# Constant products on TensorE ahead of the transposes at the block boundaries

## The reference

```python
def first_block(x, ...):
    for l in range(2):
        x = layer_norm(ALPHA * x + 0.5 * swiglu(x, ffn1...), ln_g[l, 0], ln_b[l, 0])
        proj = x @ w_in[l]                       # then pooling, gated conv, neighbourhood attention
        y = concat([y_a, y_b, y_c]) @ w_out[l]
        x = layer_norm(ALPHA * x + y, ln_g[l, 1], ln_b[l, 1])
        x = layer_norm(ALPHA * x + 0.5 * swiglu(x, ffn2...), ln_g[l, 2], ln_b[l, 2])

def second_block(x, mem, ...):
    for l in range(2):
        x = x + 0.5 * rmsnorm(swiglu(rmsnorm(x, ng[0]), w_ffn_in[l, 0], w_ffn_out[l, 0]), ng[1])
        x = x + rmsnorm(mixer(rmsnorm(x, ng[2]), ...), ng[3])   # MLA, GLA, RWKV, gates, w_out
        x = x + rmsnorm(mem_attn(rmsnorm(x, ng[4]), mem, ...), ng[5])
        x = x + 0.5 * rmsnorm(swiglu(rmsnorm(x, ng[6]), w_ffn_in[l, 1], w_ffn_out[l, 1]), ng[7])
```

## Time and profile before

| what | value |
|---|---|
| median of 3 runs | 3088.74 us (3088.4 to 3089.52) |
| the profiled execution, its own time | 3089.14 us |
| its span on the chip | 3087.2 us |
| TensorE busy (matmul) | 2788.6 us, 90% |
| VectorE, ScalarE, GpSimd busy | 1583.1, 1287.9, 477.0 us |
| mean granted TensorE clock | 0.939 |

### The profile page before, as it was taken

One profiled execution on the slowest core, in us unless ns is written; L12 is line 12 of the kernel. 1 busy time (PEld: TensorE's weight loads), 2 busy tenths in 40 slices (PEclk: granted clock), 3 DMA queues, 4 the chain that ended last, 5 costly groups with the idle time before them and its releaser, 6 DMA issues.

```text
span 3087.2 us, 52843 instructions
## 1 busy us (share of the span) xinstructions
PE 2788.6 (90%) x21412; PEld 2564.5 (83%) x21412; DVE 1583.1 (51%) x2182; ACT 1287.9 (42%) x1830; POOL 477.0 (15%) x199
## 2 busy tenths in 40 slices
PE   7989899898989989888889898998988888989898
PEld 7978798797879879777779787987977777978898
DVE  5566555555655555532555525555553254552555
ACT  3435444343544434434523444444443452344443
POOL 0000000000000000033424650000003342465000
PEclk9989999898999989898999998998989899999999
DMA  7665465566446546532322544655652232254464
GB/s 233 184 163 157 123 185 175 171 183 164 151 125 188 170 148 186 166 94 82 94 72 70 184 130 136 184 163 155 186 165 89 82 103 63 78 183 123 143 184 129
DMA packets 622823, 445.06 MB, mean 144 GB/s; under 512 B 27904, under 2 KB 589344, under 8 KB 622176
## 3 DMA queue, kind: packets, MB, share of 16 engines
q1 hardware_dynamic: 622688, 443.09, 47.8%
HBM read 441.99 MB, written 1.05 MB: 144 GB/s over the span
## 4 chain that ended last, share of the span: by engine, by line
PE 85%; DVE 9%; ACT 3%; issue 1%; DMA 1%; POOL 0%; SPq 0%; DVEq 0%; ACTq 0%; POOLq 0%
PE ps L357 18%; PE ps L358 17%; PE ps L359 17%; PE ps L373 7%; PE ps L374 7%; PE ps L375 6%; PE ps L583 2%; PE ps L607 1%; PE ps L400 1%; PE ps L1365 1%; ACT w_hi L624 1%; PE ps L1172 1%; PE ps L1079 1%; PE ps L1355 1%; DVE zT L1507 1%
## 5 line engine op out<-in xcount | busy, mean ns | idle before, releaser
L357 PE MATMUL ps<-in_hi,w_hi 128*128 128x256 f32 x4352 | 1266.8, 291 | 63.9 <-POOL w_lo L818 31.0
L358 PE MATMUL ps<-in_lo,w_hi 128*128 128x256 f32 x4352 | 1252.2, 288 | 0.0
L359 PE MATMUL ps<-in_hi,w_lo 128*128 128x256 f32 x4352 | 1250.8, 287 | 0.0
L624 ACT ACTIVATE w_hi<-raw 128x1024 fp32r<-128x1024 f32 x788 | 832.2, 1057 | 964.0 <-PE ps L359 632.8
L818 DVE TENSOR_TENSOR w_lo<-raw,w_hi 128x1024 fp32r<-128x1024 f32 x594 | 727.9, 1225 | 761.2 <-ACT w_hi L624 760.4
L357 PEld LDWEIGHTS ps<-in_hi,w_hi 128*128 128x128 f32 x4352 | 857.3, 197 | 85.9 <-issue 34.1
L358 PEld LDWEIGHTS ps<-in_lo,w_hi 128*128 128x128 f32 x4352 | 857.4, 197 | 7.1 <-issue 0.5
L359 PEld LDWEIGHTS ps<-in_hi,w_lo 128*128 128x128 f32 x4352 | 856.0, 197 | 0.0
L818 POOL TENSOR_TENSOR w_lo<-raw,w_hi 128x1024 fp32r<-128x1024 f32 x194 | 476.5, 2464 | 2357.4 <-ACT w_hi L624 2356.5
L373 PE MATMUL ps<-w_hi,hid_hi 128*128 128x512 f32 x704 | 283.3, 402 | 31.6 <-DVE hid_lo L892 31.6
L374 PE MATMUL ps<-w_lo,hid_hi 128*128 128x512 f32 x704 | 282.1, 401 | 0.0
(11 more groups left out here) (301 smaller groups left out, 2694.9 us busy)
## 6 DMA issues: line engine op xcount, KB each, us to landing
raw<-in_w_ffn_in SPq DMA_DIRECT2D x176, 512.0 KB, 3.7
raw<-in_w_mix SPq DMA_DIRECT2D x112, 512.0 KB, 3.6
raw<-in_ffn_w_gate SPq DMA_DIRECT2D x88, 512.0 KB, 3.7
raw<-in_ffn_w_up SPq DMA_DIRECT2D x88, 512.0 KB, 3.7
raw<-in_ffn_w_down SPq DMA_DIRECT2D x88, 512.0 KB, 3.5
raw<-in_w_ffn_out SPq DMA_DIRECT2D x88, 512.0 KB, 3.5
raw<-in_w_in SPq DMA_DIRECT2D x40, 512.0 KB, 4.7
raw<-in_w_out SPq DMA_DIRECT2D x32, 512.0 KB, 3.6
```

Of the source, the lines that this page charges most:

```text
L357: nc.tensor.matmul(o, lh, rh, start=first, stop=False, **kw)
L358: nc.tensor.matmul(o, lh, rl, start=False, stop=False, **kw)
L359: return nc.tensor.matmul(o, ll, rh, start=False, stop=last, **kw)
L624: nc.scalar.activation(w_hi[:, e % SPLIT, :], raw[:, e % RAW, :], ACT.Copy).then_inc(sem("split_high"), 1)
```

## The change

`pe_warm(pe, n)` runs n products of `ones` by `ones` in fp32, 128 x 128 by 256 columns, into PSUM bank 5, which nobody reads. None of them waits for a semaphore or signals one. They stand behind the block's last product and ahead of the turn, or ahead of `layer_end` and behind it. Nothing else is changed; each count holds for each of the two layers of its stack.

```diff
--- before.py
+++ after.py
@@ -386,6 +386,13 @@
 
                         mm.then_inc(sem("rows_out"), 1)
                 mm.then_inc(sem("piece_used"), 1)
+
+        WARM_BANK = 5
+
+        def pe_warm(pe, n):
+
+            for _ in range(n):
+                nc.tensor.matmul(ps[:, WARM_BANK, 0:S], ones[:, 0:P], ones[:, :], start=True, stop=True)
 
         BY_TOKENS = [(t, d) for t in range(HALF) for d in range(2)]
         BY_COLUMNS = [(t, d) for d in range(2) for t in range(HALF)]
@@ -1603,6 +1610,7 @@
             with pe.Fori(0, LAYERS) as l:
                 pe_turn(pe, 0, x_tok, BY_COLUMNS, waits=False)
                 pe_ffn(pe, 0, E1_FFN1, C1_FFN1)
+                pe_warm(pe, 9)
                 pe_turn(pe, 0, x_tok, BY_COLUMNS)
                 pe_linear(pe, 0, E1_IN, [features] * 8 + [tokens] * 2, C1_IN, TOGETHER)
 
@@ -1629,13 +1637,17 @@
 
                 pe.wait_ge(sem("na_out"), NA_HEADS)
                 pe_rows(pe, E1_OUT, C1_OUT)
+                pe_warm(pe, 9)
                 pe_turn(pe, 1, x_tok, BY_COLUMNS)
                 pe_ffn(pe, 1, E1_FFN2, C1_FFN2)
+                pe_warm(pe, 12)
                 layer_end(pe, l + 1)
 
             with pe.Fori(0, LAYERS) as l:
+                pe_warm(pe, 5)
                 pe_turn(pe, 0, z_tok, BY_TOKENS)
                 pe_ffn(pe, 0, E_FFN1, C_FFN1)
+                pe_warm(pe, 15)
                 pe_turn(pe, 1, z_tok, BY_TOKENS)
                 pe_linear(pe, Q_IN, E_IN, [features] * FIRST_SLOTS, C_IN)
                 fill = Filling(pe)
@@ -1670,8 +1682,10 @@
 
                 pe.wait_ge(sem("mem_out"), MEM_HEADS)
                 pe_rows(pe, E_O, C_O)
+                pe_warm(pe, 15)
                 pe_turn(pe, 3, z_tok, BY_TOKENS)
                 pe_ffn(pe, 1, E_FFN2, C_FFN2)
+                pe_warm(pe, 8)
                 layer_end(pe, l + 1 + LAYERS)
```

## The result

The changed kernel takes 3069.11 us (median of 5 runs, 3067.16 to 3070.5); the kernel before, run beside it, 3088.4 us (5 runs, 3081.03 to 3089.52). The ratio is 0.9941, 95% interval 0.9927 to 0.9956. That is 19.3 us less, where 16.6 us were forecast. The profiled execution after takes 3069.11 us with a span of 3067.3 us; the mean granted clock went from 0.939 to 0.960.

A forecast was written before the change was run, and what follows sets the result against it. TensorE was taken to bound the kernel, running products at half clock behind waits. Terms of -6.4, -6.2, -2.0 and -2.0 summed to -16.6 us, from 3089.14 to 3072.5, stated as 3072; range 3064 to 3086.

The forecast's parts named there:

- Which idle time lowers the clock: At TensorE's waits: about 2 us idle still holds the clock, 2.6 us loses it; read from two places.
- The price of a product: Each added fp32 128x256 product on TensorE costs 0.465 us at clock 1.00 and 0.87 us at 0.50.
- Second stack, inner boundaries: Feed-forward to mixer and rows to second feed-forward, 15 products each: clock held, 3.2 and 3.1 us saved, each twice.
- First stack, first boundary: First feed-forward to input products, 9 products: 1.0 us saved, twice; bounds 0 and 3.4; clock may fall inside the turn.
- First stack, rows: Rows to second feed-forward, 9 products: 3.6 us left idle, so 0 gained; upper bound 4.12/2 + 0.3 = 2.4, twice.
- Layer end, jump back: First stack's layer end, 12 products, once: 6.2 us left idle, so 0; the drain is not late.
- First to second stack: Boundary with 12, then 5 products, once: turn 1.3 us late but clock back earlier, -2 us; bounds -3 and +4.3.
- Second stack's jump back: Layer end with 8, then 5 products, once: the 5 cost +2.3 to +4.35, partly regained; 0, bounds -2 and +4.4.
- constant products don't hold the clock: Rival 1, at the fills: all-ones products don't count as work, so fills overrun; +12 us, 3101; chance 0.08.
- the turn loses the clock: Rival 2: the fill holds the clock but it falls in the turn, so only the turn's gains stay; 3085; chance 0.14.
- 3.6 us left is short enough: Rival 3: the first stack's second boundary gains too, 4.8 us more, 3067; chance 0.10.
- The rival on code: Rival 4: 73 added products move later TensorE instructions; one or two more stalls give back 3 to 6 us, 3077; chance 0.11.

The follow-up runs named there:

- the half fill: The change with 8 in place of 15 products at the second stack's two inner boundaries: 3082.82 us, ratio 0.9977 against the kernel before.
- the last experiment: 20 more products at the start, added to the version with fills at inner boundaries and ahead of the last `down`: 3064.89 us, 0.992 against the kernel before.

## Why the prediction was right, point by point

- **What bounds the kernel, and the mechanism:** right. The clock is 1.00 through the second stack's inner boundaries, and products behind them run at twice the rate. The kernel with only these fills, and the half fill, show that this is where most of the gain comes from.
- **Which idle time lowers the clock:** served at the second stack's inner boundaries and behind the first stack's rows, where full products that left up to 2.0 us idle held it and those that left 3.9 us or more did not. At the first stack's first boundary full products left 0 to 1.7 us where the clock held, but also 0.28 us in one pass and 1.7 to 2.0 us in five where it fell. That turn waits another 1.33 us between its halves.
- **The price of a product:** 0.43 us in place of 0.465 at 1.00, and 0.85 in place of 0.87 at the lower level.
- **Second stack, inner boundaries:** forecast 3.2 and 3.1, measured 3.05 and 3.25. The idle time left was 1.24 and 1.98 us; the second is more than the 1.7 us named, and held. The turns alone start another 0.9 and 1.1 us earlier, because the last `down` met the clock at another moment; the forecast had no term for that, and it named a clock of 1.00 from this `down` on, which mostly ran at 0.50.
- **First stack, first boundary:** 1.0 forecast, 1.5 and 1.9 measured. The term was too small, within its bounds, but the reason given for halving it was real: in six passes of four experiments with full products the clock fell inside this turn. What no term had is that attention behind it lost more than it gave.
- **First stack, rows:** 0 forecast, 0.2 and 0.8 measured. **Layer end, jump back:** 0 forecast, 0.4 measured.
- **First to second stack:** -2 forecast, -2.8 measured. The clock came back earlier, as said. The turn, forecast 1.3 us late, was late by 0.3: it starts 0.8 us behind the start of VectorE's first z columns in place of 0.5. Half of the five products still ran at 1.00, and the five took 3.4 us, not 4.35.
- **Second stack's jump back:** 0 forecast, -1.1 measured, and this is right by luck. The five products cost the 4.4 us that were named as the upper bound. I had thought part of it might fall into the stall and the clock would give back the rest. In fact the earlier clock gave 1.1, and 4.3 came with the code's place, which removed the stall. Without that the term would have been +3.3.
- **Untouched stretches:** no term. In the two traces 6.5 us are lost in attention and 4.8 in the mixer, against 7.7 gained in memory attention and the blocks around it: 3.5 us lost. The Trainium skill's rule ("TensorE: Matmul & The Clock Gate", Part 1) that the gate meets the same kernel at another phase each time was set aside for three times within 1.1 us. That was too quick: runs of the kernel before range from 3081.03 to 3095.82 us. The scatter is in such stretches and at the first stack's first boundary (0.5 to 1.9 us for the same 9 products). The second stack's inner boundaries, with 15 to 19 full products, gave 3.04 to 3.26 us in every trace.
- **The sum:** the terms of the forecast, 16.6 us, measured 21.3; the earlier turns gave 2.0 more, the untouched stretches took 3.5, and the traces differ by 19.85. Of that 4.3 are the code's place. Without them it would be 15.5 us, so the number is near for errors that partly cancel, though the greatest terms, 12.6 of the 16.6, came as forecast.
- **The rivals:** that constant products don't hold the clock is refuted by the clock in the windows. (Its sum put 0.5 us behind the rows; with the clock falling at 1878.8, as it does in the kernel before, and the same prices, it is 0.9.) That the turn loses the clock did not happen in the change, but in six passes of other kernels with full products, all at the first stack's first boundary. That 3.6 us left is short enough is refuted. The rival on code named the right mechanism with the wrong sign for this change: moving the code removed a stall, and in the last experiment brought one back.

## What to carry to other kernels

Where TensorE waits for a norm and dense products follow, look at the granted clock behind the wait: independent products can fill the wait, for a gain of half the stretch that ran at the lower level. Here 1.2 and 2.0 us left idle held the clock at the second stack's inner boundaries, and 3.9 us or more never did. Size them from the measured wait, a little short, since every product too many is paid in full, and give none to a place whose wait they cannot cover. Then look at the stretches behind as well: at one boundary the gain came with a greater loss in the next stretch. Before a gain of a few microseconds is put down to a change, run one that only moves the code by as many instructions, and take several runs: a single trace of the same code can differ by 4 us in one stretch.

## What was not expected of the hardware

- Moving TensorE's loop head by 30 products (120 instructions), with no fill near it, removed a 3.22 us stall by issue and gained 4.3 us there; a shift of 67 products made one of 4.49 us.
- Products on 64 x 64 of the array take as long as full ones (6.69 us against 6.64 us for 30 records) but in the second stack they held the clock at one of the two kinds of inner boundary only.
- The same attention code takes 88.1 to 92.5 us by the clock alone, and the long cases come almost only behind a boundary at which the clock was held. What decides where the clock falls was not tried.
- The five products' net effect (-2.2 and +3.4 us in the traces) could not be told from nothing in the medians.
